# Six buffers for sample states, w_out loaded in two parts and conditioning in pairs of slices, in a one-core hybrid decoder layer

## The reference, cut to what matters

```python
mp, ms = ada_mod(c_prompt, w_ada, b_ada), ada_mod(c_sample, w_ada, b_ada)   # silu(c) @ w + b, 6 parts of 1024
u = layer_norm(x) * (1.0 + scale) + shift                # parts 0 (shift) and 1 (scale)
x_l, g_l, z, xbc, dt_raw = split(u @ w_in)
...                                                      # RG-LRU of x_l, width-4 convolutions, silu(xbc)
def step(s, inp):                                        # SSD; for a sample row one step:
    cd, cs = inp                                         # state (16 heads x 64 x 128) decays by exp(dt * A),
    return cd[..., None, None] * s + cs, s               # takes in B * (x * dt), and gives y = C . state
y_l = rms_norm(h * gelu(g_l), lru_norm_g)
y_s = rms_norm(y * silu(z), ssd_norm_g)
out = concatenate([y_l, y_s], axis=-1) @ w_out           # 2048 x 1024
x = layer_norm(alpha * x + mp[:, 2] * out, ln1_g, ln1_b)
```

## Time and profile before

| | us |
|---|---|
| median of 3 runs | 1766.59 (1765.09 to 1768.08) |
| the profiled execution, its time | 1768.95 |
| its span, first to last instruction | 1767.2 |
| PE busy | 1546.9 (88%) |
| DVE busy | 1284.7 (73%) |
| ScalarE busy | 805.3 (46%) |
| GpSimd busy | 325.9 (18%) |

### The profile page before, as it was taken

The page is one execution under the profiler, slowest core; times in us unless marked ns, Lnnn a source line. Parts: engine busy times, 40 slices in busy tenths (PEclk is TensorE's granted clock), DMA queues, the critical chain, the costliest instruction groups (busy, mean ns, idle before and its releaser), DMA issues.

```text
span 1767.2 us, 24066 instructions
## 1 busy us (share of the span) xinstructions
PE 1546.9 (88%) x8281; PEld 1302.5 (74%) x8281; DVE 1284.7 (73%) x1392; ACT 805.3 (46%) x694; POOL 325.9 (18%) x271
## 2 busy tenths in 40 slices
PE   2899999669999983998973799999999999999872
PEld 2788989668998872876863688888888888888630
DVE  4755545478899885766766587849896788699749
ACT  2432313326565655222212356547766567577510
POOL 1000011110000000000001233323343334334200
PEclk9999999789999996999995799999999999999976
DMA  9366134344433465232330678759978787899662
GB/s 319 139 234 235 50 99 143 122 138 128 129 120 109 128 232 177 74 97 76 103 136 24 255 274 331 285 193 382 367 272 340 281 340 289 317 358 363 266 244 109
DMA packets 128284, 365.67 MB, mean 207 GB/s; under 512 B 18735, under 2 KB 89391, under 8 KB 111710
## 3 DMA queue, kind: packets, MB, share of 16 engines
q1 hardware_dynamic: 105864, 306.10, 47.4%
q0 software_dynamic: 20624, 53.36, 8.5%
q10 hardware_dynamic: 1734, 5.36, 1.0%
HBM read 332.80 MB, written 54.90 MB: 219 GB/s over the span
## 4 chain that ended last, share of the span: by engine, by line
PE 46%; DVE 6%; DMA 5%; ACT 2%; issue 2%; SPq 1%; POOL 0%; POOLq 0%; DVEq 0%; ACTq 0%
PE PS L2039 20%; PE PS L1923 10%; PE PS L2072 10%; DMA arena<-in_w_down_dram 4%; DVE low L2354 2%; ACT low L1833 2%; PE PS L2032 2%; PE PS L2105 1%; PE PS L1954 1%; PE PS L2061 1%; PE PS L1989 1%; PE PS L1946 0%; DVE st L2441 0%; DVE lower L2432 0%; DVE arena L2449 0%
## 5 line engine op out<-in xcount | busy, mean ns | idle before, releaser
L2039 PE MATMUL PS<-big 128*128 128x512 f32 x1824 | 436.1, 395 | 9.1 <-DVE big L2377 5.1
L857 PE MATMUL PS<-big 128*128 128x352 f32 x2592 | 435.7, 328 | 4.3 <-DVE big L1106 4.3
L857 PEld LDWEIGHTS PS<-big 128*128 128x128 f32 x2592 | 425.0, 191 | 13.0 <-issue 11.2
L2039 PEld LDWEIGHTS PS<-big 128*128 128x128 f32 x1824 | 342.9, 190 | 82.7 <-issue 11.7
L2354 DVE TENSOR_TENSOR big<-lower,big 128x4096 fp32r<-128x4096 f32 x64 | 283.1, 4424 | 35.9 <-ACT big L1833 34.3
L1833 ACT ACTIVATE big<-lower 128x4096 fp32r<-128x4096 f32 x64 | 232.0, 3627 | 4.6 <-DMA lower<-in_w_gate_dram 3.4
L2072 PE MATMUL PS<-low,big 128*128 128x512 f32 x912 | 224.8, 402 | 9.9 <-DVE big L2396 9.9
L2072 PEld LDWEIGHTS PS<-low,big 128*128 128x128 f32 x912 | 170.4, 190 | 49.1 <-issue 10.0
L2354 DVE TENSOR_TENSOR low<-arena,low 128x4096 fp32r<-128x4096 f32 x32 | 141.6, 4426 | 67.8 <-ACT low L1833 67.8
L1697 POOL COPY scur<-idxS 128x1 int32 x38 | 114.7, 3018 | 267.2 <-ACT arena L1866 267.2
L1833 ACT ACTIVATE low<-arena 128x4096 fp32r<-128x4096 f32 x32 | 116.3, 3634 | 82.0 <-DMA arena<-in_w_down_dram 62.5
(11 more groups left out here) (394 smaller groups left out, 1971.8 us busy)
## 6 DMA issues: line engine op xcount, KB each, us to landing
lower<-in_w_gate_dram SPq DMA_DIRECT2D x32, 2048.0 KB, 8.9
lower<-in_w_up_dram SPq DMA_DIRECT2D x32, 2048.0 KB, 8.8
arena<-in_w_down_dram SPq DMA_DIRECT2D x32, 2048.0 KB, 9.8
arena<-in_w_ada_dram SPq DMA_DIRECT2D x16, 1024.0 KB, 6.5
arena<-in_w_in_dram SPq DMA_DIRECT2D x20, 512.0 KB, 6.4
upper<-in_w_ada_dram SPq DMA_DIRECT2D x8, 1024.0 KB, 15.6
upper<-in_w_in_dram SPq DMA_DIRECT2D x16, 512.0 KB, 3.8
arena<-acs_d SPq DMA_DIRECT2D x8, 1024.0 KB
```

Source lines behind the costliest of these rows:

```text
L857: mm = pe.matmul(PS[:, 3 * b + a, 0:CH], wss[b][:, i, k, :], us[:, j, k, a * CH:(a + 1) * CH], start=(k == 0 and (i, j) == PARTS[0]), stop ...
L2039: mm = pe.matmul(PS[:, bank, :], xs[:, i, c, :], w[:, j, c, :], start=(c == 0 and (i, j) == PARTS[0]), stop=(c == KT - 1 and (i, j) == PAR ...
```

## The change

1. **Conditioning in pairs.** w_ada's first 2048 columns are loaded as four pairs (256 columns of shift and 256 of scale, `pair[c]`, two DMAs of 1 MB each), and each pair gives two slices of u: products, bias, turn, copy and scaling go pair by pair (`ada_pair(c)`, `u_pair(c)`), the first two ahead of the first projection, the third and fourth inside it, in front of slices 2 and 4. x is issued by SP and ScalarE, four tiles each, ahead of w_ada. Parameter rows, x's sample rows and b_ada (twice, in the old layout and in that of the pairs) are issued by GpSimd, 21 DMAs in front of its other constants. cT is turned first, PT1 and PT2 after all of x; the rates are worked out between u's slices 3 and 4 (`lam_rates`). The first two of w_ada's later slabs wait for PT2_MM on SP.
2. **Sample states.** Six buffers instead of three. `s_decay` stands in front of the z tiles on ScalarE and `s_step` further ahead on DVE. The EX product runs half-way through `project_split(0, 7)` instead of after `project_split(1, 7)`, the transposes for it ahead of that projection. The three new buffers lie where SEG and ER come later, so SP waits for all state steps and all six stores ahead of SEG's first load.
3. **w_out.** Only the SSD half (4 MB) is loaded in the chunk loop's tail; the LRU half is loaded after the barrier, behind the first two halves of y. Both splitting streams take y earlier among the slabs. PE waits for the router's weights at the third tile instead of the first.
4. **Decode rows.** `dpart` has a place of its own, and ScalarE's wait for `pb_mm` behind it is gone.

```diff
+        pair = [[at(23936 + 8448 * s + 2112 * c, KT, 256) for s in range(2)] for c in range(4)]
-        s0 = [at(4096 + 1024 * i, DEC, P) for i in range(3)]
+        NS = 6
+        s0 = [at(o, DEC, P) for o in (4096, 5120, 6144, A0 + 1024, A0 + 2048, A0 + 3072)]
...
+                for t in range(0, NT, 2):
+                    sp.dma_start(xt[t], x_prompt[0, t * P:(t + 1) * P, :]).then_inc(xt_loaded[t], 16)
+                def load_pair(c):
+                    for s in range(2):
+                        sp.dma_start(pair[c][s], wada_t[:, :, s * D + 256 * c:s * D + 256 * (c + 1)])\
+                            .then_inc(pair_loaded[c], 16)
+                load_pair(0)
+                load_w(COL_XBC, 0)
+                load_pair(1)
+                load_pair(2)
+                load_w(COL_XBC + P, 1)
+                load_pair(3)
+                sp.wait_ge(tensor_once, PT2_MM)
...
                     if j > 0:
                         sp.wait_ge(y_mm, j)
+                    else:
+                        sp.wait_ge(yr_ready, KT)
+                        for i in range(NS):
+                            sp.wait_ge(sn_stored[i], 16 * ((KT + NS - 1 - i) // NS))
                     sp.dma_start(SEG, ...)
...
+                def ada_pair(c):
+                    pe.wait_ge(pair_loaded[c], 32)
+                    if c > 1:
+                        pe.wait_ge(mod0_ready, c - 1)
+                    for k in range(KT):
+                        for g in range(4):
+                            mm = pe.matmul(PS[32 * g:32 * g + 32, 6 + c % 2, 0:P], cT[:, k, :],
+                                           pair[c][g // 2][:, k, P * (g % 2):P * (g % 2) + P],
+                                           start=(k == 0), stop=(k == KT - 1))
+                    mm.then_inc(ada_mm, 1)
+                    pe.wait_ge(mod0_ready, c + 1)
+                    if c > 1:
+                        pe.wait_ge(ss_ready, c - 1)
+                    pe.transpose(PS[:, 4 + c % 2, 0:P], modP[:, c, :], ident[:, :]).then_inc(ss_mm, 1)
...
+                        if by_slice and k in (2, 4):
+                            ada_pair(k // 2 + 1)
...
+                u_pair(0)
+                w_low(0, 0)
+                u_low(0)
+                u_low(1)
+                u_pair(1)
+                u_low(2)
+                u_low(3)
+                lam_rates()
+                u_pair(2)
+                u_low(4)
+                u_low(5)
+                u_pair(3)
+                w_low(1, 0)
+                u_low(6)
+                u_low(7)
```

ScalarE's and DVE's order between the z tiles, left ScalarE, right DVE (GpSimd's stores and loads follow the same order):

```
+                s_decay(0)                       |  +                s_step(0)
                 w_high(0, 8)                     |                   w_low(0, 8)
                 z_tile(0, 1)                     |                   z_tile(0, 1)
+                s_decay(1)                       |  +                s_step(1)
+                s_decay(2)                       |                   w_low(1, 8)
                 w_high(1, 8)                     |                   z_tile(1, 1)
-                s_decay(0)                       |  -                s_step(0)
-                s_decay(1)                       |  -                s_step(1)
                 z_tile(1, 1)                     |  +                s_step(2)
+                s_decay(3)                       |  +                s_step(3)
+                s_decay(4)                       |                   w_low(0, 9)
                 w_high(0, 9)                     |                   z_tile(0, 2)
-                s_decay(2)                       |  -                s_step(2)
                 z_tile(0, 2)                     |  +                s_step(4)
+                s_decay(5)                       |                   w_low(1, 9)
                 w_high(1, 9)                     |                   z_tile(1, 2)
-                s_decay(3)                       |  -                s_step(3)
-                s_decay(4)                       |  -                s_step(4)
                 z_tile(1, 2)                     |                   (ACS, TOT, DXW, acsT)
```

```
-                s_decay(5)                       |  +                s_step(5)
+                s_decay(6)                       |                   z_tile(0, 3)
+                s_decay(7)                       |                   w_low(0, 10, wraw[0])
                 z_tile(0, 3)                     |  -                s_step(5)
                 w_high(0, 10, wraw[0])           |  +                s_step(6)
-                s_decay(6)                       |  +                s_step(7)
-                s_decay(7)                       |                   z_tile(1, 3)
                 z_tile(1, 3)                     |                   w_low(1, 10, wraw[1])
                                                  |  -                s_step(6)
                                                  |  -                s_step(7)
```

```diff
+                project_split(0, 7, half_way=expand_heads)
...
+                for h in range(2):
+                    sp.dma_start(wo_raw[:, 8192 + 4096 * h:12288 + 4096 * h].rearrange("p (k n) -> p k n", k=4),
+                                 wo_t[0][:, 4 * h:4 * h + 4, :]).then_inc(wo_loaded[2 + h], 16)
...
-        dpart = at2(10240, 512)
+        dpart = at4(3584, 512)
-                        act.wait_ge(pb_mm, q + 1)
-                pe.wait_ge(wr_loaded, 64)
                 for q in range(NTT):
+                    if q == 2:
+                        pe.wait_ge(wr_loaded, 64)
```

More of the change, by code:

```diff
@@ new lines, in _ @@
+                for t in range(NT):
+                    x_turn(t)
+                pe.wait_ge(xn_ready, NT + 1)
+                pe.wait_ge(xnT_ready, NT - 1)
+                for k in range(KT):
+                    mm = pe.transpose(PS[:, 0, 8 * k:8 * k + 8],
+                                      xt[NT][:, k * P:(k + 1) * P], ident[0:DEC, 0:DEC])
+                mm.then_inc(xnT_mm, 1)
+                pe.wait_ge(rows_loaded, 16 * 9)
+                for k in range(KT):
+                    mm = pe.transpose(PS[:, 4, 42 * k:42 * k + 42], prow[:, k * P:(k + 1) * P], ident[0:42, 0:42])
@@ L844, in _ @@
+                mm.then_inc(tensor_once, 1)
+                pe.wait_ge(rows2_loaded, 16 * 3)
+                for k in range(XT):
+                    mm = pe.transpose(PS[:, 5, 29 * k:29 * k + 29], prow2[:, k * P:(k + 1) * P], ident[0:29, 0:29])
+                mm.then_inc(tensor_once, 1)
+                pe.wait_ge(vector_once, PT_READY)
+                ada_pair(0)
+                ada_pair(1)
                 PARTS = ((0, 0), (0, 1), (1, 0))
@@ L946, in _ @@
                         pe.wait_ge(thr_ready, j)
-                    project_split(0, j + 10, half_way=j)
+                    project_split(0, j + 10, half_way=lambda: chunk_products(j))
                     pe.wait_ge(xst_loaded, j * 16 + 16)
@@ L1082, in _ @@
+                step(ve.tensor_scalar(badaP[64:128, :, :], badaP[64:128, :, :], 1.0, None, ALU.add))
                 step(ve.tensor_scalar(bada4[0:64, 2, :], bada4[0:64, 2, :], 1.0, None, ALU.add))
-                for b in range(2):
-                    w_low(b, 0)
-                ve.wait_ge(ada_mm, 1)
+                ve.wait_ge(xnT_ready, NT)
                 ve.wait_ge(xnT_mm, NT + 1)
-                ve.tensor_tensor(modS[0], PS[:, 7, :], bada4[:, 0, :], ALU.add).then_inc(vector_once, 1)
@@ L1774, in _ @@
                 y_square(1)
+                for i in range(5, 8):
+                    wo_high(i)
                 for i in range(8, 13):
@@ L2196, in norms @@
                         .then_inc(v_ready, 1)
-                for i in range(4):
+                for i in range(2):
                     wo_low(i)
+                y_low(0)
+                wo_low(2)
                 y_sum(0)
-                y_low(0)
-                for i in range(4, 8):
+                for i in range(3, 5):
                     wo_low(i)
+                y_low(1)
+                wo_low(5)
                 y_sum(1)
-                y_low(1)
+                for i in range(6, 8):
+                    wo_low(i)
                 for i in range(8, 13):
```

298 lines of the change are left out of this document (133 added, 165 removed).

## The result

The changed kernel takes 1721.74 us, the median of 4 runs (1720.79 to 1723.17), against 1766.18 for the kernel before beside it: a ratio of 0.9749, 95% interval 0.9737 to 0.9761, or 44.4 us less. The forecast was 1718 (1709 to 1732). The profiled execution took 1723.17, its span is 1721.5.

The account below looks back on a forecast made before the run. TensorE is busy almost without a break except for pauses, which also lower its clock; everything touched lies before 916 us. Terms -5 - 22 - 16.5 - 4.9 = -48.4 us, from a median of 1766.59 to 1718; range 1709 to 1732.

Parts of the forecast that it names:

- Start: Conditioning up to the first projection's end: statistics begin at 8, projection ends at 69.6 instead of 74.5, -5 us.
- in by 16: Start: 4 MB of x at about 293 GB/s are in by 16, so their loads are hidden.
- rival (a): Start: slow clock in the pairs, pairs and slices twice as long (+10), so +5 instead of -5, 1728; chance 0.11.
- rival b: Start: GpSimd held up issuing DMAs while DVE normalises, 8 us late, +3 instead of -5, 1726; chance 0.06.
- States: Sample states: PE starts at 310.4 instead of 326.73, SEG subtraction at 352.5 instead of 374.92; -22 us in all.
- rival (c): Sample states: gap not closed, broadcast lands 8 us late with w_low and the z tile behind it, 1726; chance 0.08.
- w_out: w_out and output product: barrier earlier by 4.9 us, first tile behind barrier B by 11.6; whole part -16.5.
- Rival (d): Output product stays bound by weight splitting, early only at 1.2 GHz, or w_out's second half late: 8 us less, 1726; chance 0.08.
- Decode rows: y_high(8) 2.8 us earlier; pause 2.4 us, taken as too short for the clock to fall: -4.9, or -2.8 if it falls.
- (e): Start: slower than before because GpSimd's queue bounds it; needs over 3.4 us a request against 0.9; chance 0.03.
- (f): Whole kernel: all given back by several of the other rivals, no change; chance 0.02.
- from there on the duration of before: Behind the decode rows: stretches keep their duration; the forecast is wrong if stretches behind 916 change.

Follow-up runs that it names:

- rows_early: Changed kernel with PE's turns of the parameter rows (PT1, PT2) moved between x tiles 5 and 6; 1719.68 us, ratio 0.9744 to before.
- router_at_first: Changed kernel with one line moved back: PE waits for the router's weights ahead of the first tile; 1742.99 us, ratio 0.9857 to before.
- start_alone: Kernel before with only the conditioning in pairs (part 1) added; 1763.21 us, ratio 0.9983 to before.
- steps_ahead: Changed kernel with s_step(6), s_step(7) ahead of z tile (0, 3), and GpSimd's last state stores, acs_d store and clearing ahead of the last z stores; 1710.58 us.
- acs_first: Changed kernel with DVE's copies of ACS and TOT ahead of w_low(1, 9) and z tile (1, 2); 1718.81 us, ratio 0.9724 to before.
- ring_of_three: Changed kernel with three state buffers instead of six, loads of states 3 to 7 behind the stores that free them; 1728.00 us, ratio 0.9783 to before.
- all_four: Changed kernel with four reorderings: ACS copied first, state steps 6 and 7 ahead, rates late, parameter rows early; 1701.98 us, ratio 0.9638 to before.

## Why the prediction was right, point by point

By the means of the table (kernels with and without a part), the parts measured are -2.8, -20.9, -4.0 and -11.3, and -4.2, together -43.2; forecast were -5, -22, -4.9 and -11.6, and -4.9, together -48.4. All have the sign of the forecast and each is smaller, by 0.3 to 1.1 us and at the start by 2.2; the result is 3.7 us above the forecast. The mechanisms of the states, of w_out and of the decode rows were the ones forecast; at the start two errors went opposite ways.

**Start: -2.8 for -5, the largest miss.** Step by step: "can begin when cT is made, by my estimate at 8" was 10.20, for x was not there, and DVE waited again until 15.65 for the third tile; the normalisation ended at 32.8 for 29.3. So the step that failed is that the loads of x are hidden, "in by 16": the last of the four that SP issues landed at 21.1, 17.9 us behind its issue, beside GpSimd's b_ada and rows, which the estimate left out. ScalarE's first two (tiles 1 and 3) had landed at 4.8 and 6.1; DVE begins with tile 0, which SP loads. A start with ScalarE's tiles was not tried.

Between there and pair 0 I had 4.1 us for the small turns and copies; they took 5.5, in which DVE waits 3.12 us for PT1 (rows_early shows what stands in the way). The rest is the clock. The normalisation ends within 32.6 and 33.0 in all seven executions with this start, but pair 0 begins 3.5 us behind it in router_at_first, where the clock held until 34.7, 4.1 in start_alone (33.8), 5.2 in steps_ahead (32.1) and 5.5 in the other four, where it had fallen by 31.5. So the start of pair 0 spreads over 2.2 us, where the ends of the projection spread over 2.6; from pair 0 to there the seven take 33.6 to 34.4. The reading in rival (a) that groups of eight transposes hold the clock with half the time idle did not carry over: before, products of w_ada stood between them; here PE pauses for some 1.2 us between groups, and the clock fell.

Behind pair 0 the forecast had 36.2 us (33.4 to 69.6). The pairs were cheaper, 1.95 to 3.64 for 3.5 to 4; by chance what I took was the price at 1.2 GHz. Of the pauses feared in rival (a), here 2.1 to 4.0 us long, one or two cost the clock in each of the seven executions (18 matmuls in 4.5 to 4.7 us instead of 3.12). The rival's +10 did not come: from pair 0 on only pair 0 itself, a part of pair 1 (in acs_first all of it) and one or two groups of slices ran slow.

**GpSimd held up (rival b).** Its 21 requests took 11.05 us, from 2.06 to 13.1, 0.53 each and not 0.9; the first scaling on DVE began at 13.64, when all were issued, so the trace can't say what one does to the other. What it shows is the reverse: the scaling at 13.64 ran beside GpSimd's 16x1024 memset of 0.94 us (13.65) and took 1.50 us, where every later one of the changed kernel's execution takes 0.81 or 0.80. The Trainium skill, "SBUF — State Buffer", section "Who interferes with whom", says that such an operation and one of GpSimd exclude each other and that whoever issues first decides who waits. By that rule, the trace agrees: 0.81 and most of 0.94 are in the 1.50. Other executions have the other outcome as well. Where the scaling began between 13.55 and 13.90, it took 1.24 to 1.59 us and the memset 0.94 (five executions); where it began at 13.45 (rows_early) and 13.41 (ring_of_three), it took 0.81 and 0.84, and the memset 1.50 and 1.47. By the starts in the trace the scaling was up to 0.10 us ahead in some of the five too, so these starts alone do not tell who waits. It cost nothing: the third tile of x, which DVE needs next, landed at 15.2 to 15.8 either way.

**States: -20.9 for -22.** On the time scale of before, 1.9 us later than the changed kernel's own, `s_step(0)` began at 272.7 (forecast 274), ACS was turned at 310.05 (310.4) behind a pause of 3.66 (4), the SEG subtraction began at 353.3 (352.5), and the second pause was 8.74 (9). The broadcast was 1.3 us early, so rival (c) had no start. But one reason was wrong where the number was right, so the 310.4 was luck in part. I had DVE's work fill the time up to 309.4. In the profile DVE is idle for 2.45 us in front of `w_low(1, 9)`; the pause is the latency of ScalarE's high part, the low part, the z tile and the copy behind PE's own end, in this order only because the streams are written so. acs_first removes it with no work moved off DVE. In the same way the second pause was order: both last decays were made at 313.65 and DVE idled 9.32 us beside them. The projection behind the second pause runs slow in both kernels (13.19 us before, 13.88 now, 11.86 in steps_ahead), so cutting that pause from 13.77 to 8.74 us gave back nothing of the clock and lost 0.7.

**w_out: -4.0 and -11.3 for -4.9 and -11.6.** The stores land in 4.0 us instead of 8.2, the first product is at B + 7.6 (forecast B + 7.7), the first tile done at B + 32.8 (B + 33). The first term was mis-sized on paper: 8.2 less "about 4" is 4.2 and not 4.9. Rival (d) didn't come: PE's waits for slabs in the first tile were 0.36 us, and only its first 3.7 us ran at 1.2 GHz. router_at_first bears out the claim about: without the move of that wait the second term is +10.8 instead of -11.3.

**Decode rows: -4.2 for -4.9.** The pause is 2.27 (2.4). "Too short for the clock to fall, I take it" held in 5 of 10 executions. The Trainium skill, "TensorE: Matmul & The Clock Gate", section "Part 1: The HAM clock gate", says that the same kernel shows a different number of slow matmuls from run to run; the ten executions, with the same code there and an equal pause, agree: five ran slow, five did not. The right term was the mean of the two ends that I had kept, 4.9 and 2.8: 3.9.

**The rest.** Rivals (e) and (f) had no start either: requests took 0.53 us, not 3.4. And "from there on the duration of before" is true of the means, while two single executions differ by 2.7 us.

## What to carry to other kernels

When an engine's stream ends a pause, ask whether it was working or waiting in front of the instruction that counts: if it was idle, the pause is an order written by hand. Here moving one copy gave 4.4 us and moving two steps with their stores 11.8, beside some 6 for three more buffers. Wait for an operand at its first use: one wait two tiles too early would have turned 15 us won into a loss behind the barrier. Price a pause of TensorE with both clocks: of those of 2.27 us half lost it, of those of 3.66 us six in seven. And compare stretches over several executions before a difference of 2 or 3 us gets a cause.

## What the runs showed of the hardware

- A pause of 2.27 us, the same in ten executions, kept the clock at 2.4 GHz in five and lost it in five (1.7 us). A pause of 3.66 us in the states lost it in six of seven executions (1.5 to 2.3 us), pauses of 5.18 us (4 executions) each time, single pauses up to 1.00 us (acs_first, steps_ahead, all_four, in the states) never.
- Short pauses in a row cost it too: between the turns of x, at the start, PE pauses for 1.2 us in every 2.3, and there or in the small turns behind them the clock fell, first between 24.9 and 34.7, in nine of the ten executions with the new start; in all_four it held.
- The profile's clock column reads 1.00 up to its first record, but PE starts slow: with the new start the first two turns of x take 1.94 and 1.97 us in every execution, and 1.09 only from the first record on, which lies between 21.5 and 27.0.
- GpSimd issued small loads of one row in 0.50 us each, those of b_ada with many pieces in 0.6, states of 512 KB in 0.9.
- 64 PE instructions of 128 columns on a quarter of the array took 1.95 us at 2.4 GHz and 3.64 at 1.2; I had 3.5 to 4 without regard to the clock.
- A state store of 512 KB landed 3.8 to 5.8 us behind its issue in the changed kernel (median of eight 4.5), up to 7.1 in ring_of_three, where GpSimd waits 6.53 us for it. The last two y stores took 4.0 us (median) where 4 MB of w_out were loaded shortly before them, 8.3 where it was 8 MB.
